# One step of a hybrid conv/pooling/MoE trunk: the order at the end of the in-projection rewritten on four engines

## What is computed

```
h = rmsnorm(x, g_mix);  z = h @ w_in                       # parts a, g, u of 512 columns each
a = z_a * sigmoid(z_g);  u = z_u
c = silu(layernorm(causal_dwconv(a, 31 taps)))
o_a = c @ w_pw + b_pw
o_b = multiscale_pool(u, windows 2, 4, 8, 16) @ w_pool * pool_scale
x = x + concat(o_a, o_b) @ w_out
h2 = rmsnorm(x, g_ffn);  x = x + hier_moe(h2)              # 32 experts, top 2
x = x + sigmoid(rmsnorm(x) @ w_ple_gate) * (p @ w_ple_proj);  y = rmsnorm(x)
```

## Time and profile before

| | |
|---|---|
| time, median of 3 runs | 1083.68 us (1082.42 to 1083.89) |
| profiled execution, its own time | 1084.85 us |
| its span, first to last instruction | 1083.1 us |
| PE busy | 1016.2 us (94%) |
| DVE busy | 690.3 us (64%) |
| ACT busy | 458.2 us (42%) |
| POOL busy | 389.6 us (36%) |
| mean granted clock of PE | 0.971 of full |

### The profile page before, as it was taken

The page is one execution under the profiler, slowest core; times in us unless marked ns, Lnnn a source line. Parts: engine busy times, 40 slices in busy tenths (PEclk is TensorE's granted clock), DMA queues, the critical chain, the costliest instruction groups (busy, mean ns, idle before and its releaser), DMA issues. The chain is left out here.

```text
span 1083.1 us, 17645 instructions
## 1 busy us (share of the span) xinstructions
PE 1016.2 (94%) x4944; PEld 621.5 (57%) x4945; DVE 690.3 (64%) x1151; ACT 458.2 (42%) x585; POOL 389.6 (36%) x418
## 2 busy tenths in 40 slices
PE   5999996899999997999999999999999999799996
PEld 4899995777888752444444344344344344258885
DVE  5489899889222264557556646656656665667886
ACT  5445455667222132336335435425525434343332
POOL 2158785788100312333333323324233332023310
PEclk8999998799999998999999999999999999899999
DMA  9221772111223399989999999999999999956531
GB/s 281 70 59 40 223 192 106 66 59 59 79 97 123 138 412 377 401 316 361 418 419 418 420 418 416 419 418 412 418 420 418 404 418 420 412 203 213 178 133 44
DMA packets 90401, 295.08 MB, mean 272 GB/s; under 512 B 11720, under 2 KB 42500, under 8 KB 65787
## 3 DMA queue, kind: packets, MB, share of 16 engines
q1 hardware_dynamic: 75227, 263.63, 62.3%
q0 software_dynamic: 7296, 18.11, 4.8%
q10 hardware_dynamic: 7840, 12.85, 3.2%
HBM read 261.20 MB, written 37.54 MB: 276 GB/s over the span
## 5 line engine op out<-in xcount | busy, mean ns | idle before, releaser
L2153 PE MATMUL ps_gate_up<-weights,x_turned 128*64 128x512 f32 x1568 | 354.6, 603 | 14.3 <-DVE x_turned L2083 13.8
L2153 PEld LDWEIGHTS ps_gate_up<-weights,x_turned 128*64 128x64 f32 x1568 | 134.9, 139 | 225.0 <-issue 220.2
L116 ACT COPY weights<-raw_weights 128x2048 f32 x93 | 175.1, 1902 | 157.1 <-DMA raw_weights<-w_exp_gate 62.1
L2165 PE MATMUL ps_y<-weights,h_turned 128*64 128x512 f32 x784 | 179.6, 597 | 2.6 <-DVE h_turned L2093 2.6
L116 DVE COPY weights<-raw_weights 128x2048 f32 x93 | 115.3, 1240 | 78.4 <-DMA raw_weights<-w_exp_up 46.1
L466 POOL TENSOR_TENSOR conv_pool_taps<-conv_pool_taps,tap_product 128x448 f32<-128x448 f32 (+1 forms) x88 | 135.9, 1545 | 39.4 <-ACT tap_product L572 29.2
L2093 DVE STREAM_TRANSPOSE h_turned<-hidden 32x128 f32<-32x128 f32 x392 | 118.5, 302 | 33.4 <-PE ps_y L2165 28.2
L1996 POOL COPY x_tokens<-x_tokens_next 128x512 f32<-128x512 f32 x48 | 38.6, 804 | 269.2 <-DMA x_tokens_next<-h_rows,token_ids 163.9
L129 POOL DMA_INDIRECT x_tokens_next<-h_rows,token_ids x96 | 114.7, 1195 | 55.4 <-POOL token_ids L124 40.8
L2165 PEld LDWEIGHTS ps_y<-weights,h_turned 128*64 128x64 f32 x784 | 67.5, 138 | 105.3 <-issue 101.8
L917 DVE SCALAR_TENSOR_TENSOR taps_bank<-a_ext,par,taps_bank 128x640 f32<-128x640 f32 (+1 forms) x128 | 101.6, 794 | 3.3
(11 more groups left out here) (295 smaller groups left out, 1471.2 us busy)
## 6 DMA issues: line engine op xcount, KB each, us to landing
raw_weights<-w_exp_gate SPq DMA_DIRECT2D x62, 1024.0 KB
raw_weights<-w_exp_up SPq DMA_DIRECT2D x62, 1024.0 KB
raw_weights<-w_exp_down SPq DMA_DIRECT2D x62, 1024.0 KB
y_rows<-y_tile ACTq DMA_DIRECT2D x96, 128.0 KB
y_rows<-zero_rows SPq DMA_DIRECT2D x16, 512.0 KB, 6.3
x_rows<-x_tile SPq DMA_DIRECT2D x9, 512.0 KB, 2.6
h_rows<-h_tile SPq DMA_DIRECT2D x9, 512.0 KB, 2.9
late_room<-x_rows SPq DMA_DIRECT2D x9, 512.0 KB, 4.6
```

Of the source, the lines that this page charges most:

```text
L116: copy(S.work[s][:, :], raw).then_inc(S.w_ready[s], 1)
L2153: last = pe.matmul(ps_gu[side[j], :, :], x_t[:, k, :], w[:, :, c, share(D_EXP, j)], start=(k == 0), stop=(k == KD - 1))
L2165: last = pe.matmul(ps_y[side[j], :], h_t[:, k, :], w[:, share(D, j)], start=(k == 0), stop=(k == KE - 1))
```

## The change

No operation is added or removed, except that one `out_products` call becomes three calls with the same 24 matmuls. Only positions in the lists of PE, DVE, ACT and POOL move (and the two waits of `out_products` are made finer for its parts). The diff, cut to its core:

```diff
 # POOL
-                add_taps(53)
+                add_taps(51)
                 ln_pow(0)
-                add_taps(6)
+                add_taps(8)
 # ACT
-                products(3)
+                products(1)
+                conv_square(0)
+                products(2)
                 w_out_hi(0)
+                o_to_hi(0, 0, 2)
                 w_out_hi(1)
-                o_to_hi(0, 0, 1)
-                conv_square(0)
-                o_to_hi(0, 1, 2)
-                products(1)
-                w_out_hi(2)
...
                     silu(0, c)
-                o_to_hi(0, 2, 3)
+                o_to_hi(0, 3, 4)
                 products(1)
-                o_to_hi(0, 3, 4)
-                a_tail(3)
...
+                o_to_hi(0, 4, 6)
+                w_out_hi(2)
                 conv_square(1)
                 o_to_hi(0, 6, 7)
+                products(1)
+                w_out_hi(3)
+                a_tail(3)
                 products(1)
                 o_to_hi(0, 7, 8)
                 products(1)
                 side_leave()
-                products(3)
+                products(5)
                 o_to_hi(1, 0, 2)
                 products(2)
                 silu(1, 0)
 # PE
-                z_products(3, "a", 2)
...
-                    pe.wait_ge(o_left, BLOCKS * (m + 1))
+                    pe.wait_ge(o_left, BLOCKS * (m + 1) - (1 if ks[-1] < KD - 1 else 0))
                     if m == 0:
-                        pe.wait_ge(wo_split, 2 * h + 2)
+                        pe.wait_ge(wo_split, 2 * h + (1 if ks[-1] < KH else 2))
...
                 mean_products(0)
+                z_products(3, "a", 2)
                 o_products(0, 0, 2)
...
-                o_products(0, 3, 8)
+                o_products(0, 3, 7)
+                var_products(1)
+                pe.wait_ge(a_ready, KC * CHUNKS)
+                out_products(0, 0, range(KH))
+                out_products(0, 0, range(KH, KD - 1))
+                o_products(0, 7, 8)
                 pe.wait_ge(row_loaded, 80)
                 side_turn()
-                var_products(1)
-                pe.wait_ge(a_ready, KC * CHUNKS)
-                out_products(0, 0)
+                out_products(0, 0, range(KD - 1, KD))
                 broadcast(1)
...
+                out_products(3, 0)
                 mean_products(3)
-                out_products(3, 0)
```

65 lines of the change are left out of this document (28 added, 37 removed).

## The result

| | median | lowest to highest | runs |
|---|---|---|---|
| before | 1082.56 us | 1082.42 to 1083.89 | 6 |
| changed kernel | 1106.77 us | 1105.46 to 1110.76 | 6 |

The changed kernel takes 1.0219 times as long, 95% interval 1.0206 to 1.0233: 24.2 us more, where 14.3 were forecast and 1102.5 us was the end of the range. The direction was right, the size too small. The profiled execution of after took 1110.76 us, 4 us over the median, with a span of 1109.0.

What follows compares the result with a forecast made beforehand. DVE, not PE, was taken as the engine the others wait for in the front. Two ways of PE's lateness averaged +14.7 us, less 0.4, gave +14.3: 1098.0 us on the median, own range 1093 to 1102, widened to 1088 to 1102.5.

Steps and rivals of the forecast that it cites:

- The gain of PE is spent before broadcast(1): Tile 0's LayerNorm: mean_products(1) 8.6 us earlier, but only 2.3 us left at the broadcast of group 1.
- The late taps: DVE, piece 4: 17th tap 14.3 us later, out_products(1, 0) 14.4 us late, group 2's first diagonal 15.3 us late.
- the mean of the two ways, less 0.4: PE 14.4 us late one way, about 15 the other: +14.7, less 0.4 for small waits no longer met: +14.3 us.
- The split and block 7 behind it: Block 7 behind parts of out_products(0, 0): 59th sum ends at 207.3, ln_pow(1) at 208.3, group 1's broadcast at 209.1.
- The swap of group 3: out_products(3, 0) ahead of mean_products(3): less cover before turn2(2, 1), put at nothing, 1.5 us either way.
- The low clock: PE at low clock after each wait, plus a second slow sum: loss of 17 us, 1100.7, as upper bound only.
- One for one to the end: Expert weight stream and routing begin only after `front`, so what the front gains or loses reaches the end in full.
- ACT's products are held further on: Rival: products also stand ahead of o_to_hi and squares in other places; loss 18 to 24 us, about 1104; chance 0.07.
- A smaller loss: Rival: POOL and DVE catch up as POOL runs its sums without gaps; loss 3 to 9 us, about 1090; chance 0.14.
- The gain stays: Rival: DVE hardly waits, 17th tap ends at 211.2, nothing lost, up to 4 us won, 1079.7; chance 0.08.

Runs made afterwards that it cites:

- early LayerNorm: Kernel before with tile 0's LayerNorm ahead of the a products, windows ahead of most low halves, piece 4's taps ahead of add(0, 0), out_products(0, 0) whole: +3.7 us [2.2, 5.2].
- late taps: Kernel before with only DVE's taps placed where the change has them: +16.6 us [12.8, 20.3].
- swap alone: Kernel before with only out_products(3, 0) ahead of mean_products(3) and add(3, 0) ahead of centre(3): +3.0 us [1.8, 4.3].
- split: Kernel before with tile 0's LayerNorm early, plus out_products(0, 0) in three parts with block 7 and side_turn between: +9.0 us [5.4, 12.5] against before.
- Two waits filled: Changed kernel with unread matmuls in PE's waits: 6 ahead of broadcast(2), 9 + 3 x 2 ahead of o_products(1, 3): +18.2 us [15.6, 20.7] against before.
- the delayed kernel: Kernel before with 22 unread matmuls ahead of var_products(0), behind a wait for `centred`: +8.6 us [6.0, 11.2].
- three waits filled: Changed kernel with unread matmuls on PE ahead of broadcast(1), o_products(1, 3) and broadcast(2): +29.5 us [25.9, 33.1] against before.
- no swap: Changed kernel with mean_products(3) ahead of out_products(3, 0) and centre(3) ahead of add(3, 0) again: +19.7 us [17.6, 22.0] against before.
- 22 matmuls: Kernel before with 22 unread matmuls on PE ahead of var_products(0), behind a wait for `centred`: +8.6 us [6.0, 11.2].
- pow earlier: Changed kernel with ln_pow(1) two sums earlier in POOL's list: +20.9 us [18.6, 23.2] against before.

## Why the prediction was right in direction and 9 us short

**The gain of PE is spent before broadcast(1): right.** mean_products(1) came 9.0 us earlier (8.6 forecast), broadcast(1) 0.9 later where 2.3 of gain were to be left. The early LayerNorm by itself has no gain in time either. DVE was the engine waited for, and most of the hole on PE filled changed nothing. The Trainium skill, page "Perfetto Trace Analysis", section "Optimization Strategies", asks to keep the matmul engine busy and to work on what blocks it. Here the first half alone was worth -0.5 us [-2.3, +1.3] with matmuls that nobody reads and +3.7 [2.2, 5.2] with the a products; the second is where the time is.

**The late taps: right in mechanism, the size in part by luck.** Alone they put out_products(1, 0) 14.1 us and broadcast(2) 15.7 us back; forecast were 14.4 and about 15. The time is 16.6. But alone scale(1) ends at 212.7 on the old scale because DVE waits 5.02 us for PE; the forecast had it at 212.6 because DVE's own list was long. In the changed kernel it ends at 216.4, and out_products(1, 0) is 18.2 us late. The whole of the forecast was this term.

**The step that failed is the sum.** It was "the mean of the two ways, less 0.4", with every other part of the change at nothing or as a gain. Three terms were missing or too small. In the trace of after, against before: broadcast(1) is 0.9 us late where it was to be 2.3 early; broadcast(2) is 19.8 late where PE was forecast 15; broadcast(3) is 27.4 late, of which the swap alone makes 2.6; the last route is 29.0 late.

- *The split and block 7 behind it.* The prediction had the chain (block 7, side_leave, the 59th sum, ln_pow(1), "the broadcast of group 1 is then at 209.1") and ended it 3.2 us too early. On the old scale block 7's low half ends at 205.3 for 204.2, since a w_out_lo took 3.23 us and a window sum 2.23 beside POOL's sums; the 59th sum ends at 209.7 for 207.3; and the two diagonals take 1.34 us. The forecast priced one slow sum at 8.83 / 4 = 2.2 us, which is the mean of slow and fast ones: the slow ones took 3.13 and 2.99, and here 2.93. It was the 58th sum, so the 59th waited for POOL and not for side_leave: its product ended at 203.9, the 58th sum at 205.9. Measured as +5.3 between two kernels, and 3.4 us of the trace come back when the pow is moved.
- *The swap of group 3*, "I put this swap at nothing, with 1.5 us either way". It is 3.0 [1.8, 4.3]. turn2(2, 1) waits 2.54 us for ACT's h_t, 0.78 before. The cover was named, out_products(3, 0) and 5.7 us, and then taken as if it were still there.
- *The low clock.* It was in the bounds for one or two stretches, not in the sum. Two waits filled give 5.5 us back with no other edit (3.1 by the medians). This cost lies in part inside the others, since waits such as the 9.20 and 2.93 us bring it along.

These don't add up simply: late taps 16.6, early LayerNorm 3.7, split 5.3 and swap 3.0 are 28.6 against 23.7 of the whole. That 5 us overlap fits waits that cover each other ahead of o_products(1, 3), but it wasn't tested pair by pair, and the intervals of the parts are 1 to 4 us wide on each side. Moved into the waits of the changed kernel the taps give back 9.6 us and not 16.6; in that kernel the 17th tap is still 9.3 us late.

**One for one to the end: right, within a few us.** From the last route on, before takes 698.8 us and the changed kernel 698.3; the delayed kernel shows it by experiment (10.0 us at the last mark, 8.6 [6.0, 11.2] in time). In single executions this stretch took 696.1 to 705.2 us, and the place that the marks count from was reached between 170.1 and 173.5 us. That is why the 29.0 us of the last route are 25.9 of span in the same two traces: after had reached that place 2.5 us earlier, and its stretch to the end was 0.5 shorter. The change's size in time is 23.7, and the profiled execution is 4 us over the median; where in the kernel the other executions were shorter, the record doesn't show.

**The rivals.** "ACT's products are held further on" named a larger loss, 18 to 24, and the size came out at its upper end. Its mechanism did not decide: with the products behind the silus the loss stays within the interval. "A smaller loss", by POOL catching up, is out: POOL was held longer, 13.57 us. The slow sums came as the Trainium skill's page "GPSIMD Engine Reference", section "1. Specifications", has it (the two contend when VectorE has two inputs in SBUF): 2.93 us for the sum beside w_out_lo in after and 1.13 for the next, beside which DVE stood still. The prediction let the sum move by 1 to 2 us for that; in the rows DVE was slowed as well, two quarters of w_out_lo to 3.23 us each and one window sum to 2.23. "The gain stays" asked for the 17th tap to end before 211 and is out: it ended at 226.5 on the old scale.

## What to carry to other kernels

Work put off on the engine that others wait for is a debt: add up what is ahead of the last step somebody waits for, in the old list and in the new, before looking at the hole that the edit fills. Then walk the edit's other parts the same way, each by itself, and price those "at nothing" by what stood over them before and what stands there now. A merged row can hide what a meeting of two engines costs, as 8.83 us for four sums did: take the instructions one by one. And a new wait of PE can cost more than its length, because the rows behind it may run at 1.2 GHz: look at those rows' durations. Behind the one of 2.93 us the trace loses some 5 us so; filling that wait alone did not change the time clearly, filling two did.

## What was unexpected in the hardware

The low clock behind short waits. After the wait of 2.93 us a 128x512 matmul took 0.63 us until 270.8 us and 0.39 from 271.1 on; with six matmuls in the wait the same rows took 0.39, the first of them 0.48. Yet ten matmuls in the wait of 5.80 us of before won nothing: what var_products(0) was shorter by, the next wait for DVE was longer by.

A gather late in the program, y_rows into late_room, is waited for longer or shorter in a way that doesn't follow the kernel. In the view of PE's waits from 900 us (us in total, times, longest) the changed kernel has

```profile
PE ps_h3t L2446 <- DVE late_room L2356: 0.7, 2, 0.4
```

and the one with three waits filled

```profile
PE ps_h3t L2461 <- DVE late_room L2371: 5.2, 1, 5.2
```

It was 4.6 to 5.2 us in five profiled executions (late taps, swap alone, no swap, three waits filled, 22 matmuls) 2.9 in pow earlier and 0.3 to 1.1 in the other eleven. In the five the stretch from the last route to the end took 700.3 to 705.2 us, in the rest 696.1 to 699.6. That is of the size by which executions of one kernel differ here (1084.68 to 1091.01 us for the swap alone), and a reason to set marks in the front beside each time. What decides how long it is was not found.
